# A two-layer decoder trunk in split single precision: the up products of a feed-forward taken two chunks at a time, with one 2x2 block by seven products

## The chip, the cores and the metric

One core of a Trainium2 chip runs the kernel. The metric is the device time of one execution in microseconds (us); lower is better.

## What is computed

The input is x, 256 tokens of width 1024. Two layers follow, each with this shape (`rmsnorm`, mixers and attention are left as they are by the change):

```
x = x + 0.5 * swiglu_ffn(rmsnorm(x, norm_ffn1), ffn1_w_in, ffn1_w_out)     # d_ff = 2816
x = x + concat(four mixers of rmsnorm(x) @ mix_w_in) @ mix_w_out
x = x + cross_attention(rmsnorm(x), rmsnorm(mem), ...)
x = x + 0.5 * swiglu_ffn(rmsnorm(x, norm_ffn2), ffn2_w_in, ffn2_w_out)

def swiglu_ffn(h, w_in, w_out):
    g, u = jnp.split(h @ w_in, 2, axis=-1)      # the up products: 1024 -> 2 x 2816
    return (jax.nn.silu(g) * u) @ w_out         # the down products
```

There are thus four feed-forwards, two in each layer. The change touches the up products `h @ w_in` of three of them: the second of layer 0, and both of layer 1.

## The kernel before, in words

**Precision.** All matrices are float32. For the array each one is split into a high part and a low part (`w_hi`, `w_lo`, `xT_hi`, `xT_lo`), and one block product is three matmuls into the same accumulator: high by high, high by low, low by high (lines L1640, L1641, L1642 in `unit`). A block is 128x128 of the activations, held stationary, by 128x512 of the weights. "A product" below means such a block with its three matmuls.

**Units and slots.** The weights stream through three slots of `w_raw`. A unit is what fills one slot, 128x2048 floats (four k blocks of 512 columns, 1 MB). Its life: SyncE issues its DMAs once the slot is free (`unit` in the sync block, L339 waits, L341 issues; free means that the unit three before has been split); ScalarE copies it to `w_hi` (`split_hi`, L510), after the matmuls of the unit three before are done; VectorE subtracts to `w_lo` (`split_lo`, L909); TensorE multiplies. The order of all of this is written out by hand, the same order of units on each engine, and each engine runs its own queue strictly in order.

**The up stage.** A feed-forward has FC = 11 chunks of 256 hidden columns. A chunk's 512 weight columns are its 256 gate columns and its 256 linear ones. Chunk c takes units `base + 2c` (k blocks 0 to 3) and `base + 2c + 1` (k blocks 4 to 7), and both token tiles t = 0, 1 in each: 8 k blocks by 2 tiles, 16 products, 48 matmuls, into the accumulators `acc[c % 3][t]`. When tile t is complete, ScalarE makes the gate (`gate`, L562), VectorE the hidden values (`hact`, L1039) and a transpose within blocks (L1057). GpSimd then issues 16 small DMAs that finish the transposition (`shuffle`, L463), and two chunks later ScalarE and VectorE split the result into `hT` (`hidden_hi`, L581, and `hidden_lo`, L1085). For chunks 0 to 2 VectorE also forms sums of token blocks there (`token_sums`, L1092 to L1096).

**The down stage** is already done partly by seven products for a 2x2 block (`singles`, `sums`, `weight_sums`, L918 to L920). Of a unit of that kind ("singles") only three of the four 512-column parts are split, as lone parts (L507 and L508 on ScalarE, L904 and L906 on VectorE).

**Entering a feed-forward.** The last half of x is updated (`update`, L1029), TensorE transposes it (`x_turn`, L1517), VectorE scales it (`gained`, L963) and the two engines split it into `xT` (L533, L969). The first unit of the feed-forward needs the first half of x only, so it is multiplied with those transposes between its tiles; the second unit needs the other half. VectorE then splits units `base + 2` and `base + 3` one after the other, ahead of chunk 0's hidden values.

## Time and profile before

| What | us |
|---|---|
| median of 3 runs (1097.26 to 1097.81) | 1097.7 |
| the profiled execution, its own time | 1095.27 |
| its span, first to last instruction | 1093.4 |
| TensorE busy in the span | 1081.8 (99%) |
| VectorE busy | 820.2 (75%) |
| ScalarE busy | 577.0 (53%) |
| GpSimd busy | 391.8 (36%) |
| granted TensorE clock | 0.999 |

The span is what the views of the trace describe; the execution's own time is 1.9 us longer, and the median of the runs lies 2.4 us above that time. Busy time of TensorE is from matmul records whose ends are modelled and that overlap, so that the spacing of their starts, not their length, tells the rate.

### The profile page before, as it was taken

Reading aid. Unit: us, or ns where it says so; the run is one execution under the profiler, and the core shown is the slowest. Engines: PE = TensorE matmul, PEld = TensorE weight load, DVE = VectorE, ACT = ScalarE, POOL = GpSimd, SP = SyncE. Lnnn points to the kernel's source line nnn. Section 1 sums busy time; section 2 is a strip of 40 time slices with the busy share of each in tenths; the row PEclk is TensorE's granted clock in tenths of the full one; section 3 lists DMA queues with packets and bytes.
Section 4 is the critical chain, followed back from the end, with each engine's and each line's share of the span. In section 5 each row is a group of like instructions: output and inputs, shape, how many; then the busy total and the mean of one; then the engine's idle time right before and its main releaser. Section 6 shows DMA issues by size and latency. Waiting matters only on the chain.

```text
span 1093.4 us, 14359 instructions
## 1 busy us (share of the span) xinstructions
PE 1081.8 (99%) x5314; PEld 911.8 (83%) x5314; DVE 820.2 (75%) x1015; ACT 577.0 (53%) x656; POOL 391.8 (36%) x774
## 2 busy tenths in 40 slices
PE   8999999999999999999999999999999999999997
PEld 6888888889898888888878888788988988888886
DVE  6686798799767766668776667878997767666796
ACT  6454454854565544446454444567455555444544
POOL 0687722000000057673226868030000002677800
PEclk9999999999999999999999999999999999999999
DMA  8976557644553477655766764675445436666462
GB/s 277 294 246 215 167 192 256 210 155 149 197 194 116 147 219 225 210 186 182 259 214 209 229 209 150 220 249 193 154 169 187 177 123 197 217 216 217 144 222 107
DMA packets 180722, 215.94 MB, mean 197 GB/s; under 512 B 19088, under 2 KB 138540, under 8 KB 180652
## 3 DMA queue, kind: packets, MB, share of 16 engines
q1 hardware_dynamic: 155324, 200.55, 55.4%
q0 software_dynamic: 24064, 13.16, 4.4%
q10 hardware_dynamic: 1264, 1.32, 0.4%
q8 instruction: 42, 0.69, 0.3%
q14 instruction: 28, 0.23, 0.1%
HBM read 200.79 MB, written 1.05 MB: 185 GB/s over the span
## 4 chain that ended last, share of the span: by engine, by line
PE 88%; DVE 3%; DMA 3%; ACT 2%; issue 1%; POOL 1%; SPq 0%; ACTq 0%; DVEq 0%
PE acc L1640 24%; PE acc L1642 23%; PE acc L1641 23%; PE acc L1656 3%; PE acc L1657 3%; PE acc L1658 3%; PE turn L1517 2%; DMA w_raw<-in_ffn_w_out 2%; ACT w_hi L510 1%; POOL kT L463 1%; DVE w_lo L909 1%; DMA w_raw<-in_ffn_w_in 1%; PE acc L1582 1%; PE acc L1738 1%; PE acc L1737 1%
## 5 line engine op out<-in xcount | busy, mean ns | idle before, releaser
L909 DVE TENSOR_TENSOR w_lo<-w_raw,w_hi 128x2048 fp32r<-128x2048 f32 (+1 forms) x190 | 426.9, 2250 | 165.0 <-ACT w_hi L510 164.3
L510 ACT CAST w_hi<-w_raw 128x2048 fp32r<-128x2048 f32 (+1 forms) x190 | 356.2, 1875 | 195.2 <-PE acc L1642 135.1
L463 POOL DMA_DIRECT2D kT<-kT x704 | 344.3, 498 | 145.7 <-DVE kT L1057 106.8
L1640 PE MATMUL acc<-w_hi,xT 128*128 128x512 f32 x808 | 316.8, 392 | 0.0
L1642 PE MATMUL acc<-w_hi,xT 128*128 128x512 f32 x808 | 314.7, 389 | 0.0
L1641 PE MATMUL acc<-w_lo,xT 128*128 128x512 f32 x808 | 314.4, 389 | 0.0
L1642 PEld LDWEIGHTS acc<-w_hi,xT 128*128 128x128 f32 x808 | 151.7, 188 | 32.0
L1640 PEld LDWEIGHTS acc<-w_hi,xT 128*128 128x128 f32 x808 | 151.7, 188 | 31.1 <-DVE w_lo L909 0.4
L1641 PEld LDWEIGHTS acc<-w_lo,xT 128*128 128x128 f32 x808 | 151.8, 188 | 30.9
L1640 PE MATMUL acc<-w_hi,hT 128*128 128x512 f32 x432 | 170.3, 394 | 1.3 <-DVE w_lo L909 1.2
L1642 PE MATMUL acc<-w_hi,hT 128*128 128x512 f32 x432 | 168.4, 390 | 0.0
L452 POOL TENSOR_TENSOR rstd<-var,mhalf 128x2 f32<-128x2 f32 x13 | 21.7, 1666 | 409.2 <-DVE var L975 263.5
L1641 PE MATMUL acc<-w_lo,hT 128*128 128x512 f32 x432 | 168.2, 389 | 0.0
L562 ACT ACTIVATE gate<-acc,rstd 128x256 f32<-128x256 f32 x88 | 41.6, 475 | 119.5 <-PE acc L1642 119.5
L1640 PEld LDWEIGHTS acc<-w_hi,hT 128*128 128x128 f32 x432 | 81.2, 188 | 20.3 <-issue 3.9
L1642 PEld LDWEIGHTS acc<-w_hi,hT 128*128 128x128 f32 x432 | 81.1, 188 | 17.3
L1641 PEld LDWEIGHTS acc<-w_lo,hT 128*128 128x128 f32 x432 | 81.2, 188 | 15.7
L1039 DVE SCALAR_TENSOR_TENSOR hact<-acc,rstd,gate 128x256 f32<-128x256 f32 x88 | 41.9, 481 | 46.0 <-ACT gate L562 46.0
L446 POOL DMA_DIRECT2D kT<-kT x48 | 23.4, 497 | 91.5 <-DVE kT L943 91.5
L1206 DVE SCALAR_TENSOR_TENSOR arena<-arena,par_all 128x256 f32<-128x256 f32 x120 | 49.5, 480 | 0.0
L527 ACT ACTIVATE arena<-xs 128x512 f32<-128x512 f32 x34 | 21.4, 630 | 52.7 <-DVE xs L1029 52.1
L1656 PE MATMUL acc<-xT,w_hi 128*128 128x256 f32 x128 | 36.5, 285 | 0.0
(218 smaller groups left out, 1228.4 us busy)
## 6 DMA issues: line engine op xcount, KB each, us to landing
w_raw<-in_ffn_w_in SPq DMA_DIRECT2D x172, 512.0 KB, 4.8
w_raw<-in_ffn_w_out SPq DMA_DIRECT2D x80, 512.0 KB, 4.4
w_raw<-in_mix_w_in SPq DMA_DIRECT2D x32, 512.0 KB, 4.7
w_raw<-in_xattn_wkv SPq DMA_DIRECT2D x32, 512.0 KB, 4.6
kT<-kT POOLq DMA_DIRECT2D x704, 16.0 KB, 3.4
w_raw<-in_mix_w_out SPq DMA_DIRECT2D x16, 512.0 KB, 4.1
w_raw<-in_xattn_wq SPq DMA_DIRECT2D x16, 512.0 KB, 4.5
w_raw<-in_xattn_wo SPq DMA_DIRECT2D x16, 512.0 KB, 4.3
```

Of the source, the lines that this page charges most:

```text
L463: pool.dma_start(hfeat[B * q:B * q + B, g % 2, a * RUN:(a + 1) * RUN], hblk[B * a:B * a + B, g % 2, q * RUN:(q + 1) * RUN]).then_inc(hfeat ...
L510: act.copy(w_hi[:, u % SLOTS, 0:n], w_raw[:, u % SLOTS, 0:n]).then_inc(w_split_hi, 1)
L562: act.activation(gate[:, t, :], acc[c % 3][t][:, 0:HC], ACT.Silu, scale=rstd[:, V_F2 if f else V_X, t:t + 1]).then_inc(gate_ready, 1)
L909: dve.tensor_tensor(w_lo[:, u % SLOTS, 0:n], w_raw[:, u % SLOTS, 0:n], w_hi[:, u % SLOTS, 0:n].bitcast(F32), ALU.subtract).then_inc(w_spli ...
L1039: dve.scalar_tensor_tensor(out=hact[:, t, :], in0=acc[c % 3][t][:, HC:GN], scalar=rstd[:, V_F2 if f else V_X, t:t + 1], in1=gate[:, t, :], ...
L1206: ins = dve.scalar_tensor_tensor(out=cacc[:, ct, :], in0=src, scalar=tap, in1=cacc[:, ct, :], op0=ALU.mult, op1=ALU.add)
L1640: pe.matmul(o, hi, wh, start=((first is True or first == ("tile", t)) and i == 0), stop=False)
L1641: pe.matmul(o, hi, wl, start=False, stop=False)
L1642: ins = pe.matmul(o, lo, wh, start=False, stop=(last and i == nk - 1))
L1656: pe.matmul(o, w_hi[:, slot, cols], hi, start=(first and c % 2 == 0 and j == 0), stop=False, skip_group_check=True)
L1657: pe.matmul(o, w_hi[:, slot, cols], lo, start=False, stop=False, skip_group_check=True)
L1658: ins = pe.matmul(o, w_lo[:, slot, cols], hi, start=False, stop=(last and j == GK - 1), skip_group_check=True)
```

## The change

In three of the four feed-forwards (all but the first of layer 0) chunks 1 to 8 are taken in four pairs, c = 1, 3, 5, 7 with c + 1. For each pair:

- The four units hold other pieces: `u = base + 2c` holds k blocks 0 and 1 of both chunks, `u + 1` k blocks 2 to 5 of chunk c, `u + 2` k blocks 6 and 7 of both, `u + 3` k blocks 2 to 5 of chunk c + 1. Units u and u + 2 come by four DMAs of 256 KB instead of two of 512 KB.
- The 2x2x2 piece (k blocks 0 and 1, two token tiles, two chunks) is computed by seven products in place of eight. Four sums of weight blocks are formed on VectorE (`up_weight_sums`, three instructions) and split (`sums_hi` on ScalarE, `sums_lo` on VectorE, 128x2048 each). Of unit u only three parts are split, the lone ones. Four sums of token blocks are formed and split once for each feed-forward (`up_token_sums`, `up_token_hi`, `up_token_lo`).
- The seven products share partial results. The first one (`first_product`, M1) goes to x0, the accumulator of chunk c's tile 0. ScalarE copies that bank to chunk c's tile 1 (`m1_seed`), then copies the growing bank twice to SBUF (`u2_copy`, `u3_copy`), and VectorE adds these copies to the accumulators of chunk c + 1 (`m5_seed`, `u3_add`).
- TensorE issues the pair in the order of `two_chunks`, with waits on the copies and sums. The first product of a pair stands ahead of the last four products of the pair before; for the first pair it stands between the two tiles of unit `base + 1`.
- On VectorE the lone parts of the next pair's unit are split right behind the odd chunk's hidden values; the split of `base + 2` and `base + 3` moves behind the new sums at the entry.

```diff
@@ DVE, split_lo and the new sums
+                up_c = up_singles(at.l, u)[1]
+                if up_c == UP_PAIRS[0]:
+                    up_weight_sums(u, at)
                 dve.wait_ge(w_split_hi, at.at(UNITS, u + 1))
-                if e and e[0] == "singles":
+                if e and e[0] == "singles" or up_c:
...
+            def up_weight_sums(u, at):
+
+                w = w_raw[:, u % SLOTS, :].rearrange("p (i j n) -> p i j n", i=2, j=2)
+                s = t_raw.rearrange("p (c n) -> p c n", c=4)
+                dve.wait_ge(w_landed[u % SLOTS], at.at(32 * (UNITS // SLOTS), 32 * (u // SLOTS + 1)))
+                dve.wait_ge(second_k_landed, 32 * (up_pair_no(at.l, *up_singles(at.l, u)) + 1))
+                steps.link(dve.tensor_tensor(s[:, 0:2, :], w[:, :, 1, :], w[:, 0, :, :], ALU.subtract))
+                steps.link(dve.tensor_tensor(s[:, 2, :], w[:, 1, 1, :], s[:, 0, :], ALU.subtract))
+                dve.tensor_tensor(s[:, 3, :], w[:, 1, 0, :], s[:, 2, :], ALU.subtract).then_inc(ut_ready, 1)
@@ DVE, chunk
+                    if paired(l, f, c) and paired(l, f, c + 2):
+                        split_lo(base + 2 * (c + 2), at)
+                    if paired(l, f, c + 1):
+                        m5_seed(c + 1)
                     if c >= 2:
                         hidden_lo(c - 2)
+                    if paired(l, f, c) and paired(l, f, c + 2):
+                        sums_lo(c + 2)
...
+                    if paired(l, f, c + 1):
+                        first_split()
+                        u3_add(c + 1)
+                        if paired(l, f, c + 3):
+                            up_weight_sums(base + 2 * (c + 3), at)
...
+                if (l, f) != (0, 0):
+                    up_token_lo()
+                    sums_lo(UP_PAIRS[0])
+                    weights_to(base + 3, Layer(l))
                 for c in range(FC):
                     chunk(c, Layer(l))
@@ DVE, the boundary ahead of a feed-forward
                     xT_lo_part(b + 1, 0, 1, at)
+                    if g == G_FFN2:
+                        up_token_sums()
                     update(b, 1, 0, u_end + 2, pairs[1], factor, at)
@@ ACT, chunk
                         act.activation(gate[:, t, :], acc[c % 3][t][:, 0:HC], ACT.Silu,
                                        scale=rstd[:, V_F2 if f else V_X, t:t + 1]).then_inc(gate_ready, 1)
+                        if t == 0 and paired(l, f, c + 1):
+                            m1_seed(c + 1)
                     if c >= 2:
                         hidden_hi(c - 2)
-                    split_hi(base + 2 * c + 4, at)
+                    if paired(l, f, c + 1):
+                        u2_copy(c + 1)
+                    if not paired(l, f, c) or not paired(l, f, c + 2):
+                        split_hi(base + 2 * c + 4, at)
+                    if paired(l, f, c + 1):
+                        u3_copy(c + 1)
...
                     split_hi(base + 2 * c + 5, at)
+                    if paired(l, f, c + 1) and paired(l, f, c + 3):
+                        split_hi(base + 2 * (c + 3), at)
+                        sums_hi(c + 3)
@@ PE, ffn
+                def two_chunks(c):
+
+                    n = up_pair_no(l, f, c)
+                    u = base + 2 * c
+                    x0, x1 = [acc[c % 3][t][:, :] for t in range(T)]
+                    y0, y1 = [acc[(c + 1) % 3][t][:, :] for t in range(T)]
+                    pe.wait_ge(us_ready, 2 * l + f)
+                    pe.wait_ge(ut_split, n + 1)
+                    summed(y1, 0, up_sum(0), first=True)
+                    pe.wait_ge(m1_seeded, n + 1)
+                    summed(x1, 2, up_sum(1)).then_inc(m6_done, 1)
+                    plain(x0, u, 2, 1, 0)
+                    pe.wait_ge(w_split, at0.at(UNITS, SLOTS + u + 2))
+                    plain(x0, u + 1, 0, 2, 0)
+                    pe.wait_ge(u2_copied, n + 1)
+                    summed(x1, 1, up_sum(2)).then_inc(m7_done, 1)
+                    plain(x0, u + 1, 1, 3, 0)
+                    plain(x0, u + 1, 2, 4, 0)
+                    pe.wait_ge(u3_copied, n + 1)
+                    summed(x1, 3, [xT_hi[:, 1, P:2 * P], xT_lo[:, 1, P:2 * P]])
+                    pe.wait_ge(m5_seeded, n + 1)
+                    into(y0, *up_sum(3), w_hi[:, u % SLOTS, 3 * GN:], w_lo[:, u % SLOTS, 3 * GN:]).then_inc(unit_done, 2)
+                    plain(x0, u + 1, 3, 5, 0).then_inc(unit_done, 1)
...
+                    pe.wait_ge(w_split, at0.at(UNITS, SLOTS + u + 4))
+                    for t, o in enumerate((y0, y1)):
+                        for j in range(GK):
+                            ins = plain(o, u + 3, j, 2 + j, t, last=j == GK - 1)
+                        ins.then_inc(unit_done, 1)
+                        if t == 0 and paired(l, f, c + 2):
+                            first_product(c + 2)
```

**Where rows move, 1: VectorE entering a feed-forward.** From the variance to the first hidden values, entering layer 0's second feed-forward, before:

```order
@B1@
```

And with the change (`arena<-w_raw` are the sums of weights, `k_last` the low parts of the token sums, `hT<-arena` those of the weight sums):

```order
@A1@
```

The sums, the token sums' low parts and the weight sums' low parts now stand ahead of and between the splits of units `base + 2` and `base + 3`. Further up in the same queue, ahead of the update of the last half of x (`xs<-acc,xs`), the change has four small instructions, the token sums, where the kernel before has none:

```order
@A2@
```

**Where rows move, 2: TensorE at unit `base + 1` of layer 0's second feed-forward,** where tile 0 (acc00) ends and tile 1 (acc01) begins, before:

```order
L1640 MATMUL acc00<-w_hi,xT 128x512
L1641 MATMUL acc00<-w_lo,xT 128x512
L1642 MATMUL acc00<-w_hi,xT 128x512
L1640 MATMUL acc01<-w_hi,xT 128x512 [waits xT_ready]
L1641 MATMUL acc01<-w_lo,xT 128x512
L1642 MATMUL acc01<-w_hi,xT 128x512
L1640 MATMUL acc01<-w_hi,xT 128x512
```

And with the change:

```order
L1795 MATMUL acc00<-w_hi,xT 128x512
L1796 MATMUL acc00<-w_lo,xT 128x512
L1797 MATMUL acc00<-w_hi,xT 128x512
L1871 MATMUL acc10<-w_hi,xT 128x512 [waits w_split]
L1872 MATMUL acc10<-w_lo,xT 128x512
L1873 MATMUL acc10<-w_hi,xT 128x512
L1795 MATMUL acc01<-w_hi,xT 128x512 [waits xT_ready]
```

The pair's first product (acc10) stands between the tiles and waits for the split of unit `base + 2`, which before was wanted only after tile 1.

**Where rows move, 3: VectorE at chunk 3,** an odd chunk inside a feed-forward, from its hidden values (acc00, acc01) to the second of the two splits behind them, before:

```order
L1039 SCALAR_TENSOR_TENSOR hact<-acc00,rstd,gate 128x256 [waits gate_ready,hblk_ready]
L1039 SCALAR_TENSOR_TENSOR hact<-acc01,rstd,gate 128x256 [waits gate_ready]
L1092 TENSOR_TENSOR xg<-kT 128x128 [waits hT_hi_ready]
L1093 TENSOR_TENSOR xg<-kT 128x128
L1095 TENSOR_TENSOR xg<-xg,kT 128x128 [waits dve_step]
L1096 TENSOR_TENSOR xg<-kT,xg 128x128 [waits dve_step]
L1085 TENSOR_TENSOR hT<-kT,hT 128x2x256
L909 TENSOR_TENSOR w_lo<-w_raw,w_hi 128x2048 [waits w_split_hi]
L1057 STREAM_TRANSPOSE kT<-hact 128x2x2x4x32 [waits xfeat_landed,hfeat_landed0,hact_ready]
L909 TENSOR_TENSOR w_lo<-w_raw,w_hi 128x2048 [waits w_split_hi]
```

And with the change:

```order
L1158 SCALAR_TENSOR_TENSOR hact<-acc00,rstd,gate 128x256 [waits gate_ready,hblk_ready]
L1158 SCALAR_TENSOR_TENSOR hact<-acc01,rstd,gate 128x256 [waits gate_ready]
L1003 TENSOR_TENSOR w_lo<-w_raw,w_hi 128x512 [waits w_split_hi]
L1005 TENSOR_TENSOR w_lo<-w_raw,w_hi 128x1024
L1241 TENSOR_TENSOR xg<-kT 128x128 [waits hT_hi_ready]
L1242 TENSOR_TENSOR xg<-kT 128x128
L1244 TENSOR_TENSOR xg<-xg,kT 128x128 [waits dve_step]
L1245 TENSOR_TENSOR xg<-kT,xg 128x128 [waits dve_step]
L1234 TENSOR_TENSOR hT<-kT,hT 128x2x256
L1221 TENSOR_TENSOR hT<-arena,hT 128x2048 [waits ut_hi_ready]
L1182 STREAM_TRANSPOSE kT<-hact 128x2x2x4x32 [waits xfeat_landed,hfeat_landed0,hact_ready]
L1008 TENSOR_TENSOR w_lo<-w_raw,w_hi 128x2048 [waits w_split_hi]
```

The first full split is replaced by the lone parts of the next pair's unit, which moved ahead of the `hT` work, and the low parts of the weight sums (`hT<-arena`) were put ahead of the transpose.

## Rows read from the trace of the kernel before

**Rows 1.** The page, parts 1 and 4: busy time by engine, chain that ended last.
```profile
PE 1081.8 (99%) x5314; PEld 911.8 (83%) x5314; DVE 820.2 (75%) x1015; ACT 577.0 (53%) x656; POOL 391.8 (36%) x774
...
PE 88%; DVE 3%; DMA 3%; ACT 2%; issue 1%; POOL 1%; SPq 0%; ACTq 0%; DVEq 0%
```

**Rows 2.** Waits of the matmul queue, whole span: total, times, longest, us.
```profile
PE acc L1640 <- DVE w_lo L909: 1.2, 4, 0.5
```

**Rows 3.** Two chunks of layer 1: length, then busy us of PE, PEld, DVE, ACT, POOL.
```profile
621.87:643.63 21.76, 21.76 (x98) 18.02 (x97) 13.55 (x13) 10.37 (x11) 15.62 (x32) 1.00 0.70 217
```

**Rows 4.** Timeline (start us, duration us, what), matmuls entering layer 0's second feed-forward.
```profile
370.31 0.48 PE L1640 MATMUL acc<-w_hi,xT 128*128 128x512 f32 x1
...
376.36 0.39 PE L1640 MATMUL acc<-w_hi,xT 128*128 128x512 f32 x1
...
379.07 0.39 PE L1640 MATMUL acc<-w_hi,xT 128*128 128x512 f32 x1
...
384.51 0.39 PE L1640 MATMUL acc<-w_hi,xT 128*128 128x512 f32 x1
```

**Rows 5.** VectorE within one chunk, in order of time.
```profile
584.24 0.48 DVE L1039 SCALAR_TENSOR_TENSOR hact<-acc,rstd,gate 128x256 f32<-128x256 f32 x1 [1.27 <-ACT gate L562]
...
584.75 0.29 DVE L1092 TENSOR_TENSOR xg<-kT 128x128 f32<-128x128 f32 x1
...
585.69 0.68 DVE L1085 TENSOR_TENSOR hT<-kT,hT 128x512 fp32r<-128x512 f32 x1
...
586.57 2.29 DVE L909 TENSOR_TENSOR w_lo<-w_raw,w_hi 128x2048 fp32r<-128x2048 f32 x1 [0.19 <-ACT w_hi L510]
...
588.78 0.71 DVE L1057 STREAM_TRANSPOSE kT<-hact 128x512 f32<-128x512 f32 x1
```

**Rows 6.** VectorE, the down stage's sums of weights and their lone parts.
```profile
665.57 1.18 DVE L918 TENSOR_TENSOR w_raw<-w_raw 128x1024 f32<-128x1024 f32 x1
...
668.12 0.69 DVE L904 TENSOR_TENSOR w_lo<-w_raw,w_hi 128x512 fp32r<-128x512 f32 x1
...
668.72 1.22 DVE L906 TENSOR_TENSOR w_lo<-w_raw,w_hi 128x1024 fp32r<-128x1024 f32 x1
```

**Rows 7.** VectorE entering the second feed-forwards, layer 0 and (last row) layer 1.
```profile
367.76 0.69 DVE L1029 SCALAR_TENSOR_TENSOR xs<-acc,xs 128x512 f32<-128x512 f32 x1
...
376.36 4.50 DVE L909 TENSOR_TENSOR w_lo<-w_raw,w_hi 128x2048 fp32r<-128x2048 f32 x2
...
913.82 4.50 DVE L909 TENSOR_TENSOR w_lo<-w_raw,w_hi 128x2048 fp32r<-128x2048 f32 x2
```

**Rows 8.** Matmuls entering layer 1's first feed-forward.
```profile
549.60 0.66 PE L1517 MATMUL turn<-ident,xs 128*128 128x128 f32 x4 [0.15 <-DVE xs L1029]
...
559.05 0.39 PE L1640 MATMUL acc<-w_hi,xT 128*128 128x512 f32 x1
```

**Rows 9.** VectorE entering layer 1's first feed-forward.
```profile
548.86 0.68 DVE L1029 SCALAR_TENSOR_TENSOR xs<-acc,xs 128x512 f32<-128x512 f32 x1
...
558.32 4.49 DVE L909 TENSOR_TENSOR w_lo<-w_raw,w_hi 128x2048 fp32r<-128x2048 f32 x2
```

**Rows 10.** Groups: evacuations of one bank by ScalarE, additions on one by VectorE.
```profile
L717 ACT COPY kT<-acc 128x512 f32<-128x512 f32 x8 | 4.5, 587 | 6.4 <-PE acc L1658 6.4
...
L1029 DVE SCALAR_TENSOR_TENSOR xs<-acc,xs 128x512 f32<-128x512 f32 x30 | 20.2, 685 | 2.2 <-PE acc L1642 2.2
```

**Rows 11.** DMA issues: engine, count, KB each, median us from issue to landing.
```profile
w_raw<-in_ffn_w_in SPq DMA_DIRECT2D x172, 512.0 KB, 4.8
...
w_raw<-in_ffn_w_out SPq DMA_DIRECT2D x16, 256.0 KB, 2.9
```

**Rows 12.** A matmul that follows a wait, in the down stage.
```profile
501.18 0.47 PE L1640 MATMUL acc<-w_hi,hT 128*128 128x512 f32 x1 [0.23 <-DVE w_lo L909]
```

**Rows 13.** ScalarE around the first gate of layer 0's second feed-forward.
```profile
376.61 1.92 ACT L510 CAST w_hi<-w_raw 128x2048 fp32r<-128x2048 f32 x1 [1.16 <-PE acc L1642]
...
379.31 1.28 ACT L562 ACT_TABLE_LOAD   x1 [0.78 <-PE acc L1642]
```

More of the change, by code:

```diff
@@ L69, in down, with up_singles @@
                 return f, DOWN[u - base]
+        return None, None
+    def up_singles(l, u):
+        for f, base in enumerate((U_F1I, U_F2I)):
+            if base <= u < base + 2 * FC and u % 2 == base % 2 and paired(l, f, (u - base) // 2):
+                return f, (u - base) // 2
         return None, None
@@ L355, in wide_parts, with two_chunk_parts @@
                         for i in range(2)]
+            def two_chunk_parts(u, src, l, a, c):
+                dst = w_raw[:, u % SLOTS, :].rearrange("p (k c g n) -> p k c g n", k=2, c=2, g=2)
+                return [(dst[:, k, :, g, :],
+                         src[l, :, a + k, g * FF + c * HC:g * FF + (c + 2) * HC].rearrange("p (c n) -> p c n", c=2))
+                        for k in range(2) for g in range(2)]
             def square_parts(u, src, l, a):
@@ L386, in ffn @@
                 at = Layer(l)
+                f = 1 if base == U_F2I else 0
                 for c in range(FC):
+                    if paired(l, f, c):
+                        u = base + 2 * c
+                        pieces = two_chunk_parts(u, src_in, l, 0, c)
+                        unit(u, at, pieces[:2])
+                        for dst, src in pieces[2:]:
+                            sp.dma_start(dst, src).then_inc(second_k_landed, 16)
+                        unit(u + 1, at, pair_parts(u + 1, src_in, l, 2, c * HC, c * HC + FF))
+                        pieces = two_chunk_parts(u + 2, src_in, l, 6, c)
+                        unit(u + 2, at, pieces[:2])
+                        for dst, src in pieces[2:]:
+                            sp.dma_start(dst, src).then_inc(last_k_landed, 16)
+                        unit(u + 3, at, pair_parts(u + 3, src_in, l, 2, (c + 1) * HC, (c + 1) * HC + FF))
+                    if (l, f) != (0, 0) and (c in UP_PAIRS or c - 1 in UP_PAIRS):
+                        continue
                     for j in range(2):
@@ L1047, in first_split @@
                             extra(EXTRA[c])
-                    if c < FC - 1:
+                    if c < FC - 1 and not paired(l, f, c + 1) and not (paired(l, f, c) and paired(l, f, c + 2)):
                         first_split()
@@ L1154, in _ @@
                         xT_lo_part(0, 1, t, at)
-                weights_to(3, at)
+                weights_to(2 if l else 3, at)
                 ffn(l, U_F1I, 0)
@@ L1712, in ffn, with into, plain @@
                 b = 3 if f else 0
+                def into(o, s_hi, s_lo, w_h, w_l, first=False, last=False):
+                    pe.matmul(o, s_hi, w_h, start=first, stop=False, skip_group_check=True)
+                    pe.matmul(o, s_hi, w_l, start=False, stop=False, skip_group_check=True)
+                    return pe.matmul(o, s_lo, w_h, start=False, stop=last, skip_group_check=True)
+                def plain(o, u, at_w, k, t, first=False, last=False):
+                    cols = slice(at_w * GN, (at_w + 1) * GN)
+                    rows = slice(t * P, (t + 1) * P)
+                    return into(o, xT_hi[:, k, rows], xT_lo[:, k, rows], w_hi[:, u % SLOTS, cols], w_lo[:, u % SLOTS, cols], first, last)
@@ new lines, in up_sum, with summed, first_product @@
+                def up_sum(i):
+                    return [us_parts[:, i // 2, q, (i % 2) * P:(i % 2 + 1) * P] for q in range(2)]
+                def summed(o, at_w, stationary, first=False):
+                    cols = slice(at_w * GN, (at_w + 1) * GN)
+                    return into(o, *stationary, t_hi[:, cols], t_lo[:, cols], first)
+                def first_product(c):
+                    u = base + 2 * c
+                    pe.wait_ge(w_split, at0.at(UNITS, SLOTS + u + 1))
+                    plain(acc[c % 3][0][:, :], u, 0, 0, 0, first=True).then_inc(m1_done, 1)
@@ L1718, in ffn @@
                     unit(base, at0, 0, xT_hi, xT_lo, 0, True, False, before=xT_wait(b, 0, at0), between=first_between)
-                    unit(base + 1, at0, 0, xT_hi, xT_lo, GK, False, True, before=xT_wait(b, 1, at0))
+                    unit(base + 1, at0, 0, xT_hi, xT_lo, GK, False, True, before=xT_wait(b, 1, at0),
+                         between=lambda t: None if t else first_product(UP_PAIRS[0]))
                 for c in range(1, FC):
+                    if (l, f) != (0, 0) and (c in UP_PAIRS or c - 1 in UP_PAIRS):
+                        if c in UP_PAIRS:
+                            two_chunks(c)
+                        continue
                     if (l, f, c) == (0, 0, 1):
```

99 lines of the change are left out of this document (92 added, 7 removed).

## The prediction

> **What bounds the kernel now.** I read the busy times first: TensorE is busy for 99% of the span and is 88% of the chain that ended last [rows 1]. Then the waits of its queue: after the start nearly none is left, 1.2 us in four waits for VectorE's splits [rows 2]. So time is matmuls times their spacing, and any wait that the change puts in front of a matmul is added in full. Next the spacing: 24 matmuls of 512 columns start from 379.07 to 384.51, 0.2267 us each [rows 4]; the 0.39 us of a record is an overlapping latency, not a price. Last the engines that feed it: in 21.76 us, two chunks, VectorE is busy for 13.55 us and ScalarE for 10.37, at clock 1.00 [rows 3]. VectorE has 8.2 us to spare in two chunks, and the change spends most of that.
>
> **What is removed.** One product of 32 in each pair: 3 matmuls, 4 pairs, 3 feed-forwards, 36 matmuls. TensorE waits for nothing in these chunks, so all of it counts: 36 x 0.2267 = 8.16 us [rows 4]. A pair now takes 31 products x 0.68 = 21.1 us.
>
> The Trainium skill, "TensorE: Matmul & The Clock Gate", section "Back-to-back issue gap", gives about 131 ns per matmul at N = 512 for a sustained stream of loads and matmuls. By that page the 36 would be worth an estimated 4.7 us, and the sum below would come out at +2.6 us instead of -0.8. The trace disagrees with it, 0.2267 against 0.131, and I go by the trace.
>
> **What is added inside the pairs (at nothing, and how tightly).** VectorE gets per pair: three sums of weights, 2.55 us (665.57 to 668.12) [rows 6]; the low parts of the sums, as long as a full split, 2.29 [rows 5]; two additions on a bank of PSUM, taken as the nearest row, 0.69 each [rows 10]. Splitting three parts instead of four saves 2.29 - 1.82 (668.12 to 669.94) = 0.47 [rows 5, 6]. 13.55 + 2.55 + 2.29 + 1.37 - 0.47 = 19.3 us in 21.1. It fits, by 1.8 us, less where a chunk also has token sums (0.94, 584.75 to 585.69) [rows 5]. Fit is not enough, since the queues are in order, so I walked the three queues through the pairs with these durations, start S being the pair's second product. The tightest pair is that of chunks 5 and 6, because chunk 1's token sums fall before it. VectorE starts hidden values at S - 7.6, has the lone parts done at S - 4.7 (M1 wants them at S - 3.4), the hT work and token sums at S - 3.3, the sums' low parts at S - 0.95 (wanted at S), the transpose, then unit u + 1 at S + 1.9 (wanted at S + 2.04, three products in). Margins 1.3, 0.95 and 0.15 us: no wait, but the last is thin. For the other pairs it is 0.4 to 1.7 us. Behind VectorE's late transpose wait GpSimd's 16 DMAs; their result is wanted two chunks later, with over 3 us to spare.
>
> ScalarE gets a split of the sums and three copies of a bank per pair; the copy's nearest row is PSUM to SBUF, 0.59 us [rows 10]. PSUM to PSUM (`m1_seed`) isn't in the trace; I take 0.59 too, with 0.48 below and 0.69 above (VectorE's price on a bank) [rows 10]. ScalarE's load is 10.4 + 1.9 + 1.8 - 0.4 = 13.7 of 21.1 us. What counts is the handshake: the second product ends at S + 1.36, its result is readable some 0.2 us later, the copy is done at S + 2.15 and wanted at S + 2.72, margin 0.57. The third copy has a full split in front of it (S + 2.0 to 3.9), is done at S + 4.4 and wanted at S + 4.76, margin 0.3. No wait again.
>
> Two units of a pair come in four transfers of 256 KB. Such a transfer lands in 2.9 us, one of 512 KB in 4.8 (medians) [rows 11]. The lone unit's slot is free when unit u + 1 is split, and by the walk VectorE wants its data 7.4 us later. It is 1 MB either way; between 4.8 and 5.8 us (two lots of 2.9, one behind the other) it isn't late. I take nothing. Two more DMAs to issue cost SyncE a fraction of a us, and its queue is idle between units.
>
> **What is added at the entries (this decides).** In-order queues make the first pair different: its sums can't be made ahead.
>
> - Entering the second feed-forwards. VectorE starts on unit base + 2 at 376.36, and 2.55 us of sums now precede the lone parts: 668.72 + 1.22 - 665.57 = 4.37 us in all, so M1 may start at 376.36 + 4.37 + 0.04 = 380.77 [rows 6, 7]. TensorE is there, after tile 0 of unit base + 1, at 379.07 [rows 4]. Wait: 1.70 us, twice (layer 1's entry shows the same split at 913.82, as long) [rows 7]. The four token sums (0.94) ahead of the update at 367.76 cost nothing there: the update would end at 369.4, the first matmuls that need it come at about 370 [rows 4, 7].
> - Entering layer 1's first. There the update at 548.86 is what TensorE waits for at 549.60 [rows 8, 9], so 0.94 us goes on the path. TensorE then reaches M1 at 559.05 + 0.94 = 559.99 [rows 8]; VectorE's chain starts at 558.32 and ends at 558.32 + 4.37 + 0.04 = 562.73 [rows 6, 9]. Wait: 2.74 us. I keep 558.32, since what VectorE waited for just before was ScalarE, whose split of that unit becomes shorter by a quarter; at worst it moves by the 0.94 too.
> - Behind M1, tile 1 takes 2.7 us, in which the two low parts (0.69 + 2.29) are nearly all done; then two products pass before unit base + 3 is wanted. Margins 0.4 to 0.6. In the second feed-forwards ScalarE has also a table load of 1.28 us in front of the first gate and the first seed [rows 13]; by the walk the seed is ready just when it is wanted, within 0.1 us.
> - A matmul behind a wait is 0.08 us longer (0.47 against 0.39) [rows 4, 12]: three times, 0.24.
>
> **The sum:** -8.16 + 2 x 1.70 + 2.74 + 0.94 + 0.24 = -0.84 us. The change earns 8.2 us in twelve pairs and gives 7.3 back at three entries. Against the profiled execution's 1095.27 us that is 1094.4; the median of the runs is 2.4 us above it, so I forecast 1097.7 - 0.8 = 1096.9. A difference under 0.2% (2.2 us) is one that a measurement here can't tell from none, so this is no change. Bounds of the main case: entry chains 0.5 us shorter or 0.94 longer, seeds at their ends, 1095.4 to 1099.0.
>
> **The rivals.**
>
> 1. *The copies are late at every pair* (slower). The margin of 0.3 us before the eighth product rests on 0.59 us per copy and 0.2 us from matmul to ScalarE. Each 0.1 us beyond it costs 12 x 0.1. With copies and handshakes 0.2 us longer the walk gives 1.9 us more, 1098.8; with 0.4 us longer 7.1 more, 1104.0. For it: a thin margin met twelve times, and copies that read a bank between matmuls. Against it: 0.59 is measured eight times. It decides from 0.25 us. Chance 0.11.
> 2. *The lone units land late* (slower). If landing takes 8 us instead of under 7.4, VectorE's sums start late, and at 92% load it catches up slowly: the walk gives 1.4 us per feed-forward, 4.3 us more, 1101.2. For it: the DMA share is 0.70 here already [rows 3]. Against: 4.8 us median [rows 11]. Chance 0.09.
> 3. *The clock falls at the entries* (slower). The array is at 1.00 throughout [rows 3], its upper level of 2.4 GHz, with hardly an idle moment [rows 2]. The change makes one of 2.7 us. If the grant fell to 1.2 GHz, 512 columns would take twice as long: at most 0.2267 us more for each of some 15 matmuls up to the next wait, 3.4 us per entry, 1100.3 if only the longest does it. The Trainium skill, "TensorE: Matmul & The Clock Gate", section "Part 1: The HAM clock gate", says that an array left idle falls back to 1.2 GHz. Chance 0.03.
> 4. *The entries cost little* (faster). If VectorE reached the lone parts on time, only 0.94 would be left: -7.2, 1090.5. A gain that shows needs 1.4 us of the 6.1 us of waits to vanish. Against it: the order of rows and durations that repeat to 0.01 us. Chance 0.13.
> 5. *A saved matmul is worth less than its spacing* (slower). At 0.13 us, a little over half of it, the 36 would bring 4.7 us: 3.4 us more, 1100.3. Against it: the spacing repeats for 24 matmuls in a row with nothing else in the queue [rows 4]. Chance 0.02. It is what the page cited above would make of them.
>
> That the change doesn't drop the matmuls can be excluded: its queue has 36 rows fewer.
>
> **How the numbers follow.** Main case 0.62, of which 0.02 ends beyond +2.2 us; the rest as above. Faster 0.13; slower 0.02 + 0.11 + 0.09 + 0.03 + 0.02 = 0.27; same 0.60. The range takes the main case's bounds, on the upper side the second rival and the milder half of the first; below it ends at half a us under the main bound, since of the fourth rival only the small part is near: 1095.0 to 1101.3.
>
> **What would show it.** Right: 5278 matmuls; three waits of TensorE for the lone split at L1003/L1005, two near 1.7 us and one near 2.7, one of about 1 us for the update at layer 1's entry; no wait above 0.1 us inside pairs; VectorE busy 19 of 21 us there; clock 1.00. Wrong: waits at `u3_copy` in every pair (first rival), VectorE waiting for DMA at the sums (second), a clock below 1 behind an entry (third), or no waits at the entries (fourth).

## The result, and the profile after

The changed kernel takes 1099.22 us (median of 20, 1097.66 to 1102.22) beside 1097.26 us (median of 20, 1094.80 to 1099.16) of the kernel before in the same runs: ratio 1.0021, 95% interval [1.0014, 1.0027], some 2 us slower. The forecast was 1096.9 us, no change that a measurement can tell. The value lies inside the range; the forecast's direction was wrong. The profiled execution after has a span of 1097.6 us, 4.2 more than before; only part of that belongs to the change, as the stretches below show.

From the page after, the busy times, the granted clock in 40 slices, and the chain that ended last:

```profile
PE 1077.7 (98%) x5278; PEld 905.0 (82%) x5278; DVE 884.2 (81%) x1114; ACT 614.7 (56%) x719; POOL 390.7 (36%) x774
...
PEclk9999999999999999999999999999999999999999
...
PE 79%; DVE 7%; ACT 5%; DMA 4%; POOL 3%; issue 2%; SPq 0%; ACTq 0%; DVEq 0%
```

36 matmuls fewer than before [rows 1], as forecast, and a smaller share of TensorE in the chain. The waits of TensorE after (beside [rows 2]):

```profile
PE acc L1871 <- DVE w_lo L1005: 6.1, 3, 2.9
PE acc L1795 <- DVE w_lo L1008: 4.1, 6, 1.4
PE acc L1679 <- POOL ident L482: 2.1, 1, 2.1
PE acc L1775 <- DVE w_lo L1048: 0.5, 1, 0.5
PE turn L1672 <- DVE xs L1148: 0.4, 1, 0.4
```

The first row is new: three waits, 6.1 us, on the split of the lone weight parts (the second row is taken up below the table). Here they are in TensorE's timeline after, with their first matmuls; [rows 4] and [rows 8] are the same places before. Number in brackets: idle time ahead.

```profile
381.57 0.50 PE L1871 MATMUL acc<-w_hi,xT 128*128 128x512 f32 x1 [1.57 <-DVE w_lo L1005]
...
562.84 0.50 PE L1871 MATMUL acc<-w_hi,xT 128*128 128x512 f32 x1 [2.91 <-DVE w_lo L1005]
...
921.44 0.50 PE L1871 MATMUL acc<-w_hi,xT 128*128 128x512 f32 x1 [1.58 <-DVE w_lo L1005]
```

VectorE's rows at the first of them, after (beside [rows 7]): three sums, then the two lone parts, a chain of 377.11 to 381.52, 4.41 us long where 4.37 was forecast.

```profile
377.11 1.22 DVE L1017 TENSOR_TENSOR arena<-w_raw 128x1024 f32<-128x1024 f32 x1
378.37 0.69 DVE L1018 TENSOR_TENSOR arena<-w_raw,arena 128x512 f32<-128x512 f32 x1
379.09 0.69 DVE L1019 TENSOR_TENSOR arena<-w_raw,arena 128x512 f32<-128x512 f32 x1
379.70 0.68 DVE L1003 TENSOR_TENSOR w_lo<-w_raw,w_hi 128x512 fp32r<-128x512 f32 x1
380.30 1.22 DVE L1005 TENSOR_TENSOR w_lo<-w_raw,w_hi 128x1024 fp32r<-128x1024 f32 x1
```

The entries, then, are as forecast. What isn't is inside the pairs. I cut both traces at the same matmuls (by their place in TensorE's order) and took the differences of their start times, in us:

| stretch | before | after | forecast difference | measured |
|---|---|---|---|---|
| first block product delayed, second feed-forwards | 8.76 | 10.50, 10.51 | +1.78 each | +1.74, +1.75 |
| the same, layer 1's first | 9.04 | 11.83 | +2.82 | +2.79 |
| ahead of it, the residual update | | | +0.94 | +0.21 |
| M1 to the pair's own start, one product more | 2.72 | 3.54 to 3.56 | +0.68 each | +0.82 to +0.85 |
| a pair, 93 matmuls for 96 (9 of them) | 21.76 | 21.27 (6), 21.39, 21.40, 21.43 | -0.68 each | -0.33 to -0.49 |
| a feed-forward's last pair, 90 for 96 (3) | 21.76 | 20.58, 20.58, 20.59 | -1.36 each | -1.18 |

("M1 to the pair's own start" runs from the first product, M1, to the pair's second.) The forecast adds up to -0.84 us here, the measured stretches to +1.4. The other 2.8 of the 4.2 us lie outside: 0.8 ahead of the first stretch that the change touches, the rest in the down stages, which it leaves as they are, and behind them. There lie 3.8 of the 4.1 us in the second row of the waits, on full splits, where [rows 2] has 1.2. That row differs between executions: it is 1.7 to 3.6 us in the seven other traces of kernels with four pairs (e1, e4, e8, e9, e11, e12, e13), and 2.2 in e2, which has the down stages of the kernel before. So it isn't shown to be the change's.

No pair is as short as 31 products of 0.68 us, although TensorE's list of waits has nothing between them. How a pair begins, TensorE's timeline after:

```profile
427.57 0.40 PE L1873 MATMUL acc<-w_hi,xT 128*128 128x512 f32 x1
427.81 0.39 PE L1871 MATMUL acc<-hT,k_last 128*128 128x512 f32 x1
428.04 0.40 PE L1872 MATMUL acc<-hT,k_last 128*128 128x512 f32 x1
428.28 0.39 PE L1873 MATMUL acc<-hT,k_last 128*128 128x512 f32 x1
428.51 0.39 PE L1871 MATMUL acc<-hT,k_last 128*128 128x512 f32 x1
428.74 0.40 PE L1872 MATMUL acc<-hT,k_last 128*128 128x512 f32 x1
428.98 0.39 PE L1873 MATMUL acc<-hT,k_last 128*128 128x512 f32 x1
429.21 0.40 PE L1871 MATMUL acc<-w_hi,xT 128*128 128x512 f32 x1
```

Six matmuls in 1.40 us (427.81 to 429.21), 0.233 each, where [rows 4] has 0.2267. This goes on for 12 products, 0.690 to 0.700 us each, and then the spacing is 0.2267 to the pair's end: 0.19 us in each of twelve pairs, 2.25 in all. That is the largest part of the forecast's error, and its cause was open.

### The profile page after: what moved, and what is told of

It is laid out like the page before. It is cut to its first block, busy times and chain, and to the rows that moved or that the text cites. A ratio compares the mean times of both kernels' runs of the same rounds, so it can differ in the third digit from the quotient of the medians.

```text
span 1097.6 us, 14533 instructions
## 1 busy us (share of the span) xinstructions
PE 1077.7 (98%) x5278; PEld 905.0 (82%) x5278; DVE 884.2 (81%) x1114; ACT 614.7 (56%) x719; POOL 390.7 (36%) x774
## 4 chain that ended last, share of the span: by engine, by line
PE 79%; DVE 7%; ACT 5%; DMA 4%; POOL 3%; issue 2%; SPq 0%; ACTq 0%; DVEq 0%
PE acc L1795 13%; PE acc L1797 13%; PE acc L1796 13%; PE acc L1871 8%; PE acc L1872 8%; PE acc L1873 8%; PE acc L1811 3%; PE acc L1812 3%; PE acc L1813 3%; ACT w_hi L562 3%; DVE w_lo L1008 3%; POOL kT L511 3%; DMA w_raw<-in_ffn_w_in 2%; PE turn L1672 2%; DMA kT<-kT 1%
## 5 line engine op out<-in xcount | busy, mean ns | idle before, releaser
L1008 DVE TENSOR_TENSOR w_lo<-w_raw,w_hi 128x2048 fp32r<-128x2048 f32 (+1 forms) x178 | 398.6, 2242 | 109.9 <-ACT w_hi L562 109.6
L562 ACT CAST w_hi<-w_raw 128x2048 fp32r<-128x2048 f32 (+1 forms) x178 | 333.0, 1873 | 157.3 <-PE acc L1797 65.6
L511 POOL DMA_DIRECT2D kT<-kT x704 | 345.2, 499 | 149.0 <-DVE kT L1182 107.3
L1795 PE MATMUL acc<-w_hi,xT 128*128 128x512 f32 x424 | 167.5, 395 | 0.3 <-DVE w_lo L1008 0.3
L1797 PE MATMUL acc<-w_hi,xT 128*128 128x512 f32 x424 | 165.4, 390 | 0.0
L1796 PE MATMUL acc<-w_lo,xT 128*128 128x512 f32 x424 | 165.0, 389 | 0.0
L1871 PE MATMUL acc<-w_hi,xT 128*128 128x512 f32 x312 | 122.3, 392 | 6.1 <-DVE w_lo L1005 6.1
L1872 PE MATMUL acc<-w_lo,xT 128*128 128x512 f32 x312 | 122.0, 391 | 0.0
L1873 PE MATMUL acc<-w_hi,xT 128*128 128x512 f32 x312 | 121.5, 389 | 0.0
L1797 PEld LDWEIGHTS acc<-w_hi,xT 128*128 128x128 f32 x424 | 79.6, 188 | 17.0
L1795 PEld LDWEIGHTS acc<-w_hi,xT 128*128 128x128 f32 x424 | 79.6, 188 | 16.5 <-DVE w_lo L1008 0.7
L1796 PEld LDWEIGHTS acc<-w_lo,xT 128*128 128x128 f32 x424 | 79.7, 188 | 15.9
L1871 PEld LDWEIGHTS acc<-w_hi,xT 128*128 128x128 f32 x312 | 58.5, 188 | 20.4 <-DVE w_lo L1005 7.3
L1873 PEld LDWEIGHTS acc<-w_hi,xT 128*128 128x128 f32 x312 | 58.6, 188 | 12.6
```

Of the source, the lines that this page charges most:

```text
L511: pool.dma_start(hfeat[B * q:B * q + B, g % 2, a * RUN:(a + 1) * RUN], hblk[B * a:B * a + B, g % 2, q * RUN:(q + 1) * RUN]).then_inc(hfeat ...
L562: act.copy(w_hi[:, u % SLOTS, 0:n], w_raw[:, u % SLOTS, 0:n]).then_inc(w_split_hi, 1)
L1008: dve.tensor_tensor(w_lo[:, u % SLOTS, 0:n], w_raw[:, u % SLOTS, 0:n], w_hi[:, u % SLOTS, 0:n].bitcast(F32), ALU.subtract).then_inc(w_spli ...
L1795: pe.matmul(o, hi, wh, start=((first is True or first == ("tile", t)) and i == 0), stop=False)
L1796: pe.matmul(o, hi, wl, start=False, stop=False)
L1797: ins = pe.matmul(o, lo, wh, start=False, stop=(last and i == nk - 1))
```

## The experiments

The traces are compared stretch by stretch; a pair of 93 matmuls at 0.2267 would be 21.08 us, the last one of a feed-forward (90) 20.40. A wait is exposed where TensorE has nothing else to do, and a clean pair is one without an exposed wait. Of e5, e8, e9, e12 and e13 there is one execution each: their stretches are compared, not their times.

### Waits, copies, or the order: e1 and e2

In e1 the five waits inside a pair are out of TensorE's queue. The copies and additions stay as work, but read other banks and write where nobody reads, so the values of the paired chunks are left incomplete:

```diff
-act.copy(acc[c % 3][1][:, :], acc[c % 3][0][:, :]).then_inc(m1_seeded, 1)
+act.copy(arena[:, 7 * GN:8 * GN], tb[0][:, :]).then_inc(m1_seeded, 1)
...
-pe.wait_ge(m1_seeded, n + 1)
...
-pe.wait_ge(u2_copied, n + 1)
...
-pe.wait_ge(u3_copied, n + 1)
...
-pe.wait_ge(m5_seeded, n + 1)
...
-pe.wait_ge(u3_added, n + 1)
```

> The changed kernel with the five waits of TensorE on the copies and additions of partial sums taken out (M1's sum, U2, M5's sum, U3 and the addition behind it). ScalarE's three copies and VectorE's two additions per pair stay in their places in the queues and in size, but read two PSUM banks of the turns and write where nobody reads, so the values of the paired chunks are left incomplete. Measured in the changed kernel: a pair takes 21.43 or 21.27 us (the last 20.58) where 93 (90) matmuls of 226.7 ns are 21.08 (20.40), 0.19 to 0.35 too much, 12 times. Theory A (a wait of TensorE costs even where it isn't exposed: the matmuls behind a condition that came true only shortly before are spaced 231 ns rather than 226.7, some 12 of them): pairs of 21.08 and 20.40 us, and some 2.3 to 2.7 us less in all, ratio to the kernel before 0.9997. Rival B (the copies and additions themselves slow the matmuls beside them by their PSUM traffic): pairs stay at 21.27 to 21.43 us, ratio 1.002. Rival C (the matmuls of the pair's order, two accumulators by turns and new operands, are slower by themselves): pairs stay too, and the slow ones keep their places in the order.

1098.12 us, ratio 1.0017 [1.0008, 1.0026]. Ten of the twelve pairs keep their length to 0.01 us, 21.27 and 20.58 (one of chunks 5 and 6 its 21.39); only the first pairs of the second feed-forwards fall, from 21.43 and 21.40 to 21.27, where the first seed had come late, by 0.05 us or less. Theory A expected 21.08 in all of them and falls. The copies' waits cost 0.3 us in all. Rivals B and C stay open here.

In e2 the kernel before gets waits that aren't needed, in front of another product in each chunk:

```diff
+                        if fresh and fresh[0] == nk * t + i:
+                            pe.wait_ge(gate_ready, fresh[1])
...
+                        fresh = None if c < 2 or (l, f) == (0, 0) else (c - 1, at0.at(4 * FC, 2 * FC * f + 2 * (c - 1) + 2))
```

> The kernel before, nothing left out, with one added wait of TensorE in each chunk 2 to 8 of the three feed-forwards that the change pairs (21 waits): on the gate of the previous chunk's second tile, which ScalarE ends about 0.8 us behind that chunk's last matmul. The wait stands before product c - 1 of chunk c, so 0.68 us later in each chunk: margins of about -0.1, 0.6, 1.2, 1.9, 2.6, 3.3 and 3.9 us. Chunks 9 and 10 have none. Before, every chunk takes 10.88 us. Theory A (a condition that came true only shortly before slows the next 12 or so matmuls to 231 ns): chunks 2 to 4 grow by 0.05 to 0.2 us each (chunk 2 by the exposed 0.1 too), those with margins over some us by nothing, sum +0.3 to +1 us. Rivals B and C (a wait that isn't exposed is free): only chunk 2 grows, by about 0.1 us, sum +0.3 us or less. If every wait costs whatever its margin, all seven grow alike.

Ratio 1.0006 [0.9995, 1.0016]. In all three feed-forwards chunk 2 grows by 0.19 us, and chunks 3 to 8, with margins from 0.6 us up, by 0.00. The rows of chunk 2:

```profile
393.46 0.39 PE L1644 MATMUL acc<-w_hi,xT 128*128 128x512 f32 x1
393.74 0.50 PE L1642 MATMUL acc<-w_hi,xT 128*128 128x512 f32 x1
394.07 0.39 PE L1643 MATMUL acc<-w_lo,xT 128*128 128x512 f32 x1
```

A wait that isn't exposed is free here; one that is late by some 0.05 us costs 0.19, since the next matmul comes after 0.33 us and the six behind it are a few ns wide too. This prices the thin margins of the prediction, but doesn't explain the clean pairs.

### Only three pairs: e3

The pairs become (3, 4), (5, 6), (7, 8). The first pair's weight sums go beside chunk 0, its other sums and M1 beside chunks 1 and 2.

```diff
-    UP_PAIRS = (1, 3, 5, 7)
+    UP_PAIRS = (3, 5, 7)
...
+                    if (l, f) != (0, 0) and c == UP_PAIRS[0] - 3:
+                        up_weight_sums(base + 2 * UP_PAIRS[0], at)
```

> The changed kernel, nothing left out, with pairs (3,4), (5,6), (7,8) alone: the chunks 0, 1 and 2 are computed as before, the first pair's weight sums are made beside chunk 0, its other sums and the first block product beside chunks 1 and 2. 9 pairs rather than 12: 27 matmuls of 226.7 ns fewer than before, -6.12 us. Theory A with the entries as the loss that the change does not win back: the waits on the weight parts at the three entries (1.74 + 2.79 + 1.75 = 6.3 us in the changed kernel) are gone, the pairs keep their 0.19 us each (+1.7) and the stretch ahead of the first its 0.15 (+0.45): -6.12 + 1.7 + 0.45 = -4.0 us, ratio 0.9964. If the longer down stages of the changed kernel (+0.18, +1.05, +0.94 us) are its own work and not spread between executions, -1.8 us, ratio 0.998. If the entries only move the wait to the first pair (its weight parts late again), about 1.000.

1092.62 us beside 1095.83, ratio 0.9971 [0.9960, 0.9982]. Chunk 0 takes what it took before, chunks 1 and 2 with M1 22.44 (21.76 + 0.68), the pairs 21.27 and 20.58 again. TensorE's waits have no row on the split of the lone parts any more (L1004 here); the two largest rows behind the start's are:

```profile
PE acc L1797 <- DVE w_lo L1007: 1.8, 3, 0.7
PE turn L1674 <- DVE xs L1147: 1.5, 1, 1.5
```

So three pairs earn and no entry gives back: the three entries' 6.3 us had bought three pairs worth 2.0 at most.

### Where the stationary operand lies: e4, e5, e8, e9, e12, e13

With the waits gone (e1), the steps over 0.2267 us began anew at products 0, 1, 4 and 8 of a pair, each followed by some unevenly wider steps, called the ripple below. These four products load the token sums from `k_last`; product 7, also one of the new scheme but with its stationary operand in `xT`, didn't start a ripple. `k_last` is the last allocation of the kernel, at byte 221984 of each partition, 32 past a multiple of 64; `xT` (byte 98432) and `hT` start on one. The places follow from the order and sizes of the allocations in the kernel. In e4 one line moves:

```diff
+        k_last = sb("k_last", [P, 2, 2, S], F32R)
         par_all = sb("par_all", [P, L, N_PAR])
...
-        k_last = sb("k_last", [P, 2, 2, S], F32R)
```

> The changed kernel, nothing left out, with one allocation moved: k_last, which holds the token sums, now stands ahead of the parameters at byte 209664 of each partition, a multiple of 64, rather than behind them at byte 221984, which is 32 past one. With the waits gone a pair still took 21.27 us, and its slow matmuls begin at the products 0, 1, 4 and 8 of a pair: the four whose stationary operand lies in k_last. Theory D (loading a stationary operand that starts 32 bytes off a 64-byte boundary takes some ns more than fits beside the matmul ahead): pairs of 21.08 and 20.40 us, save where a wait is exposed; 0.19 us off each of 12 pairs, 2.3 us less than the changed kernel, ratio to the kernel before about 1.000. Rival C' (block products that are new in the pair, alternating accumulators, are slow wherever their operands lie): no change, pairs at 21.27, ratio 1.002.

Ratio 1.0017 [1.0007, 1.0027], beside 1.0021 [1.0014, 1.0027] of the changed kernel. Clean pairs take 21.22 and 20.53: a quarter of what Theory D asked (0.05 of 0.19 us a pair). Their ripple has changed; product 4 of a pair in e4:

```profile
409.50 0.40 PE L1873 MATMUL acc<-w_hi,xT 128*128 128x512 f32 x1
409.73 0.40 PE L1871 MATMUL acc<-hT,k_last 128*128 128x512 f32 x1
409.97 0.40 PE L1872 MATMUL acc<-hT,k_last 128*128 128x512 f32 x1
410.20 0.40 PE L1873 MATMUL acc<-hT,k_last 128*128 128x512 f32 x1
```

The step behind the first load from `k_last` is 0.24 us, and after 0.045 us of excess the stream is back at 0.2267: three times per pair, 0.14.

e5 asks the same of the kernel before, where nearly every matmul then has such an operand:

```diff
+        sb("pad_a", [P, 8])
         xT = sb("xT", [P, KT, 2, S], F32R)
         hT = sb("hT", [P, FT, 2, S], F32R)
+        sb("pad_b", [P, 8])
```

> The kernel before, nothing left out, with 32 bytes of padding ahead of xT and 32 behind hT: the stationary operands of the up and down projections then start 32 bytes off a 64-byte boundary, all else keeps its place modulo 64. Before, a chunk of 48 matmuls takes 10.88 us, 226.7 ns each. Theory D: matmuls of 231 to 236 ns throughout, a chunk of 11.1 to 11.3 us, and some 4500 matmuls times 5 to 8 ns, 22 to 36 us more in all. Rival C': no change, chunks of 10.88 us, within 2 us of the kernel before.

1115.32 us (one run) beside 1095.64: +19.7, a little under the range of Theory D and far from its rival. Every two chunks take 22.40 us instead of 21.76, 0.2333 for each matmul:

```profile
399.96 0.40 PE L1642 MATMUL acc<-w_hi,xT 128*128 128x512 f32 x1
400.19 0.40 PE L1643 MATMUL acc<-w_lo,xT 128*128 128x512 f32 x1
400.43 0.40 PE L1644 MATMUL acc<-w_hi,xT 128*128 128x512 f32 x1
400.66 0.40 PE L1642 MATMUL acc<-w_hi,xT 128*128 128x512 f32 x1
```

So 32 bytes off costs 6.6 ns per matmul, shown; but in the pairs it explains 0.05 of 0.19. The rest asked for other places. e8 and e9 move the same line, `k_last` directly behind `xT` (byte 114816) and behind `hT` (159872).

> The changed kernel, nothing left out, with k_last allocated directly behind xT, at byte 114816 of each partition (a multiple of 64), rather than 221984. At byte 209664 a pair still took 21.22 us (21.08 are 93 matmuls of 226.7 ns): a matmul spaced 241 ns and a ripple behind it, 0.045 us together, at each of the products 0, 4 and 8, which fetch their stationary operand from k_last after one from xT. Theory E (the place of the operand in the partition decides, by distance from xT or by region): pairs of 21.08 us. Rival F (the kind of product or its waits decides, wherever the operand lies): 21.22 us.

> The changed kernel, nothing left out, with k_last directly behind hT, at byte 159872 (a multiple of 64). Theory E by distance from xT: between 21.08 and 21.22 us a pair; by region (the last part of the partition alone is dear): 21.08. Rival F: 21.22 us.

Both: pairs of 21.08 and 20.40 us, wherever no wait is exposed; the three with an exposed wait take 21.28 to 21.31. The same pair start in e8:

```profile
405.10 0.39 PE L1873 MATMUL acc<-w_hi,xT 128*128 128x512 f32 x1
405.32 0.39 PE L1871 MATMUL acc<-hT,k_last 128*128 128x512 f32 x1
405.55 0.39 PE L1872 MATMUL acc<-hT,k_last 128*128 128x512 f32 x1
405.78 0.39 PE L1873 MATMUL acc<-hT,k_last 128*128 128x512 f32 x1
406.00 0.39 PE L1871 MATMUL acc<-hT,k_last 128*128 128x512 f32 x1
406.23 0.39 PE L1872 MATMUL acc<-hT,k_last 128*128 128x512 f32 x1
406.46 0.39 PE L1873 MATMUL acc<-hT,k_last 128*128 128x512 f32 x1
406.68 0.39 PE L1871 MATMUL acc<-w_hi,xT 128*128 128x512 f32 x1
```

1.36 us for six, with the same instructions, waits and copies as after. The kind of product (rivals C and F) and the traffic of the copies (rival B) are excluded. e12 and e13 ask whether distance or region counts, with `k_last` ahead of the arena (184448), and behind it with `xg`, `gate` and `hact` moved behind both (201472).

> The changed kernel, nothing left out, with k_last ahead of the arena, at byte 184448 (a multiple of 64); at 114816 and 159872 a pair took 21.08 us, at 209664 it took 21.22. If the extra grows with the distance from xT (98432 to 114816): 21.1 to 21.2 us. If one region at the end of the partition is dear, and it begins above this place: 21.08 us; if it begins between 159872 and here: 21.22 us.

> The changed kernel, nothing left out, with the arena ahead of xg, gate and hact, and k_last between the arena and them, at byte 201472 (a multiple of 64). Region theory: 21.22 us, the same ripple as at 209664, if the region begins below this place, 21.08 if it begins above it. Distance theory: between the value at 184448 and 21.22.

e12: clean pairs of 21.08; e13: 21.22, with e4's ripple. The cost is none up to 188544 (e12's end of `k_last`) and full from 201472 on, and it does not grow with distance below. So these runs show a place at the end of the partition to be dear as the source of a stationary operand after loads from lower down. Where between the two it begins is open, and so is why; nor do they tell a region from a distance beyond some bound (e12's place is 86016 bytes from the start of `xT`, e13's 103040).

### The changed kernel with k_last near xT, timed: e11

> The changed kernel with k_last directly behind xT once more, now timed; nothing left out. In its first trace 9 of the 12 pairs ran at the forecast 21.08 and 20.40 us, and the sum of all stretches that the change touches was -0.8 us against the kernel before, as forecast. If the place of k_last was the whole of the forecast's error, ratio 0.9993, an interval that holds 1.000 or lies just below it, and not that of the changed kernel, 1.0021 [1.0014, 1.0027]. If the change costs something else outside these stretches (the down stages, which the profiles showed up to 1 us longer), 1.001 to 1.002.

1096.13 us beside 1095.70, ratio 1.0006 [0.9995, 1.0016]. By the centres the place is worth 0.15%, some 1.6 us, against 1.0021 of the changed kernel (its interval, [1.0014, 1.0027], overlaps this one a little; the lengths of the pairs don't), and without it the change is what was forecast, within 0.2% of the kernel before. The medians differ by +0.4 us, 1.3 above the forecast's -0.8; this has a candidate in the traces. With the change, the clock sometimes falls at the longest entry wait. TensorE's timeline of e13 at layer 1's first entry, then windows of the same trace (length, busy time and count of TensorE, its loads, VectorE, ScalarE, GpSimd, then the granted clock):

```profile
561.25 0.72 PE L1871 MATMUL acc<-w_hi,xT 128*128 128x512 f32 x1 [2.91 <-DVE w_lo L1005]
561.77 0.63 PE L1872 MATMUL acc<-w_lo,xT 128*128 128x512 f32 x1
562.20 0.63 PE L1873 MATMUL acc<-w_hi,xT 128*128 128x512 f32 x1
```

```profile
558.00:561.20 3.20, 0.34 (x2) 0.00 (x0) 3.13 (x6) 1.71 (x1) 0.00 (x0) 1.00 0.00 0
561.20:564.80 3.60, 3.55 (x9) 2.78 (x10) 3.60 (x3) 2.86 (x4) 0.00 (x0) 0.53 0.61 183
564.80:568.00 3.20, 3.20 (x15) 2.61 (x14) 2.28 (x3) 0.48 (x2) 0.00 (x0) 1.00 0.47 152
```

After 2.91 us without a matmul the next eight start 0.43 us apart (the first step is 0.52), at a mean grant of 0.53, so at the 1.2 GHz level for nearly all of that window; then it is back at 1.00. From M1 to the pair this stretch takes 5.14 us rather than 3.54: +1.6. It is so in e1, e9 and e13 (4.89, 5.11, 5.14) and not in the changed kernel's own trace, e4, e8, e11 and e12, with the same wait each time: three of eight. The waits of 1.6 us never did it. The Trainium skill, "TensorE: Matmul & The Clock Gate", section "Part 1: The HAM clock gate", has an idle array fall back to 1.2 GHz; these traces agree for three of eight such pauses. The mean granted clock of the timed executions goes the same way: it is 0.997 or less in 26 of 55 with four pairs (after, e1, e4, e11), in 1 of 71 of the kernel before and in none of the 29 with three pairs (e3, e6, e7, e10), which have no such pause. So lower grants come with the four-pair form. Three of eight at 1.5 us would be an estimated 0.6 us on the average execution. In e11 the seven executions at 0.997 or less take 1.1 us more on average than the other five, in the 20 of the changed kernel the eight 1.0 more than the other twelve, in e1 1.4, but in e4 nothing. That this closes e11's gap is argued, not shown.

### Versions that beat both: e6, e7, e10

e6 is e3 with e4's line, e7 adds the token sums of layer 1's first feed-forward behind the update, e10 is e7 with `k_last` behind `xT`.

```diff
-                    up_token_sums()
                 if l < L - 1:
                     update(3, 1, 0, U_F2O + D_LAST[1], F2O_PAIR[1], 0.5, at)
+                    up_token_sums()
```

> Pairs (3,4), (5,6), (7,8) alone, as in the run before of that form, and k_last on a 64-byte boundary; nothing left out. That form measured 0.9971 of the kernel before with k_last where it was. Theory D: 9 pairs times 0.19 us less, -1.7 us, ratio 0.9955. Rival C': 0.9971 again.

> The kernel of the run above, with the token sums of layer 1's first feed-forward made behind VectorE's next residual update rather than ahead of it; nothing left out. In the form with three pairs TensorE waits 1.5 us there for that update (turn <- xs). If the sums ahead of the update are what it waits for (the 0.94 us of the prediction, four operations), that wait falls by up to 0.94 us, ratio 0.0005 to 0.0009 lower than without the move; if the wait is set by the DMA or the additions ahead, it stays at 1.5 us.

> Pairs (3,4), (5,6), (7,8), k_last behind xT, token sums of layer 1's first feed-forward behind the update; nothing left out. With k_last at 209664 this form measured 0.9969 [0.9954, 0.9983], and its pairs took 21.22 us. Theory E: 9 pairs of 21.08, 1.3 us less, ratio about 0.9955; rival F: 0.9965, the mean of the three forms with pairs from chunk 3 so far.

e6: 0.9963 [0.9950, 0.9976], pairs 21.22. e7: 0.9969 [0.9954, 0.9983]; the wait for the update is 0.9 us, 1.7 in e6, but the same wait is 0.15 us before [rows 8] and 1.2 in e2, which is the same kernel there, 0.4 after, 1.5 in e3 and below 0.1 in e8, so it differs between executions by more than the move could bring. Its effect isn't shown. e10: 1090.11 us beside 1095.53, ratio 0.9957 [0.9943, 0.9970], pairs of 21.08 and 20.40 all through. It has the lowest ratio of all, 4.7 us below the kernel before, though its interval overlaps those of e3, e6 and e7. Its 27 fewer matmuls are worth 6.1.

## Why the prediction was wrong

- *"36 x 0.2267 = 8.16 us"*: right. 5278 matmuls, and in e8 each clean pair is shorter by exactly three (six) spacings. The rival on their worth (0.13 us each) is excluded; so is, for this stream, the 131 ns of the Trainium skill, "TensorE: Matmul & The Clock Gate", section "Back-to-back issue gap".
- *"A pair now takes 31 products x 0.68 = 21.1 us"*: this step failed, with *"what is added inside the pairs (at nothing)"*. It gave the new block products the spacing of rows whose stationary operand lies in `xT`, while four of them load from `k_last`. Measured 21.27; with `k_last` lower in the partition 21.08 (e8, e9, e12). 12 x 0.19 = 2.25 us, of which 0.6 for the 32 bytes (e4) and 1.7 for the region. The number of matmuls removed was right; the spacing of twelve products in each pair was not.
- *The entries, 1.70, 2.74, 1.70 us*: right, 1.57, 2.91 and 1.58 as waits and 1.74, 2.79, 1.75 as stretches with their restart. Removing them (e3) gives them back.
- *Token sums ahead of the update, 0.94*: 0.2 in that execution. This wait varies by over a microsecond between traces, so neither number says much.
- *The seed "ready just when it is wanted, within 0.1 us"*, and *unit u + 1 at a margin of 0.15*: both came late by 0.05 us or less, the seed in two pairs, the unit in one. With the step of 0.34 us behind a late wait that is 0.14 us each, and the three stretches behind M1 gave 0.47 more: 0.9 in all, which the shortfall of 0.8 at the entries (most of it the token sums) happened to cancel: that is luck.
- *Copies late at every pair* (first rival): no; e1 shows 0.3 us in all. *Lone units late* (second rival): its sign came, its cost didn't. VectorE waits at the sums for the transfer four times (transfers of 256 KB landed in a median of 3.8 us, not 2.9), yet the pairs that these sums feed are clean. The one pair whose unit u + 1 was late comes next after the one fed behind the longest of them; that it follows from it is not shown.

```profile
DVE arena L1017 <- DMA w_raw<-in_ffn_w_in: 2.8, 4, 1.3
```

- *Entries cost little*: no, three waits of 6.1 us.
- *The clock falls* (third rival, 0.03): its mechanism is real, in three of eight traces and at the longest entry alone. It was priced at 3.4 us an entry and takes 1.3 to 1.6. A chance of 0.03 was too small for a pause over five times as long as the longest of [rows 2].

So -0.84 + 2.25 = +1.4 is what the stretches of one execution show. The medians differ by 1.96 us, with an interval of 1.5 to 3.0. The clock, with an estimated 0.6, would bring +2.0, but agreement that close says little: terms of 0.9 and 0.8 cancelled by luck, and stages that the change leaves alone differ between executions by as much as the whole effect.

## What to carry to other kernels

Where time is a stream of matmuls, price a new matmul by a row that has its operands where the new one will have them, and look at the start times, not at the list of waits: two to three per cent on twelve products show in no list. Allocate what TensorE loads as a stationary operand first, on multiples of 64 bytes, ahead of large scratch; here the place cost twelve pairs 2.25 us, over a quarter of what the change saved. And where a block scheme needs operands made ahead, leave its first pair out if its making falls into an entry: three pairs here earned more than four.

## What the hardware showed that was not expected

- A stationary operand 32 bytes off a multiple of 64: 233.3 instead of 226.7 ns per matmul of 512 columns, through a whole kernel (+19.7 us).
- A stationary operand at byte 201472 or 209664 of a partition, after one from `xT`: a step of 241 ns and 0.045 us in all each time (e13, e4); at 114816, 159872 and 184448 nothing (e8, e9, e12).
- A wait late by some 0.05 us costs 0.19; one met with 0.6 us to spare nothing (e2).
- The clock falls to its lower level at the same pause of 2.9 us in three profiled executions of eight, for some eight matmuls; at pauses of 1.6 us in none of sixteen. Why one such pause does it and another doesn't is open.
